# Positions and half of the first weights loaded first, the residual sum placed between the last query transposes, and the last down weights and the output in pieces

## The reference, cut to what matters

```python
# block 1: x + merged @ w_out, from three attention branches; two of them rotate by position angles
cos_a, sin_a = rope_tables(positions, A_ROT)
kv_m = rms_norm(mem, g_mem) @ w_mem_kv
# block 2
h = h + _mixer(...)
# cross attention
q = _rmsnorm((u @ w_q).reshape(b, s, 4, 256), qn)
k = _rmsnorm(kv[..., :d].reshape(b, m, 4, 256), kn)
h = h + (softmax(q @ k.T / 16) @ v) @ w_out
# experts
hid = silu(xb @ w_gate[e]) * (xb @ w_up[e])      # 1024 -> 512, for the rows routed to e
h = h + gate * (hid @ w_down[e])                 # 512 -> 1024
```

## Time and profile before

| | us |
|---|---|
| median of 3 runs | 1191.72 |
| lowest and highest run | 1190.08, 1197.29 |
| profiled execution | 1191.71 |
| its span, first to last instruction | 1189.8 |
| TensorE busy | 967.1 |
| vector engine busy | 314.9 |
| ScalarE busy | 174.0 |

### The profile page before, as it was taken

One profiled execution on the slowest core, in us unless ns is written; L12 is line 12 of the kernel. 1 busy time (PEld: TensorE's weight loads), 2 busy tenths in 40 slices (PEclk: granted clock), 3 DMA queues, 4 the chain that ended last, 5 costly groups with the idle time before them and its releaser, 6 DMA issues.

```text
span 1189.8 us, 10271 instructions
## 1 busy us (share of the span) xinstructions
PE 967.1 (81%) x4175; PEld 485.3 (41%) x4176; DVE 314.9 (26%) x835; ACT 174.0 (15%) x380; POOL 39.6 (3%) x93
## 2 busy tenths in 40 slices
PE   7999998899999899999899899756566565656555
PEld 3445484754444446455544555312131212121211
DVE  2316915623110421423654434101010101010100
ACT  2114223432000012211221222000000000000000
POOL 1012110000100010100000000000000000000000
PEclk9999999989999999999899999968697878697878
DMA  9455242303440744433206737999999999999993
GB/s 325 132 174 180 106 142 81 132 1 141 142 141 1 249 146 146 170 105 140 72 1 215 284 142 283 420 429 427 427 429 427 427 428 429 426 429 429 426 427 128
DMA packets 61981, 290.23 MB, mean 244 GB/s; under 512 B 8743, under 2 KB 11630, under 8 KB 49646
## 3 DMA queue, kind: packets, MB, share of 16 engines
q1 hardware_dynamic: 61934, 289.57, 61.5%
HBM read 288.51 MB, written 1.05 MB: 243 GB/s over the span
## 4 chain that ended last, share of the span: by engine, by line
PE 62%; DMA 28%; DVE 4%; SPq 3%; issue 1%; ACT 1%; DVEq 0%; ACTq 0%
PE ACC L480 32%; PE AUX L946 7%; DMA ring<-in_w_e_gate_dram 5%; PE ACC L494 5%; DMA ring<-in_w_e_down_dram 5%; PE ACC L513 4%; PE AUX L971 3%; DMA SQE<-in_w_e_up_dram 3%; DMA BIG<-in_w_e_up_dram 3%; DMA SQE<-in_w_e_down_dram 2%; DMA PJ<-in_w_e_up_dram 2%; DMA PJ<-in_w_e_down_dram 2%; DMA BIG<-in_w_e_gate_dram 2%; PE ACC L849 2%; DMA SQE<-in_w_e_gate_dram 2%; PE AUX L524 2%
## 5 line engine op out<-in xcount | busy, mean ns | idle before, releaser
L480 PE MATMUL ACC<-ring,BIG 128*128 128x512 f32 (+2 forms) x736 | 314.0, 587 | 4.1 <-ACT R L1280 2.5
L480 PEld LDWEIGHTS ACC<-ring,BIG 128*128 128x128 f32 x736 | 140.6, 192 | 169.7 <-issue 162.4
L946 PE MATMUL AUX<-ring,R 128*32 128x512 f32 x416 | 117.0, 727 | 52.2 <-DMA BIG<-in_w_e_up_dram 20.2
L480 PE MATMUL ACC<-ring,R 128*128 128x512 f32 (+1 forms) x232 | 100.9, 593 | 3.3 <-DMA ring<-in_w_mem_kv_dram 2.0
L946 PE MATMUL AUX<-R 128*32 128x512 f32 x112 | 63.5, 732 | 23.1 <-DMA ring<-in_w_e_gate_dram 13.0
L946 PE MATMUL AUX<-BIG,R 128*32 128x512 f32 x192 | 55.4, 742 | 27.7 <-DMA PJ<-in_w_e_up_dram 20.9
L971 PE MATMUL AUX<-ring,BIG 128*32 128x512 f32 x192 | 54.2, 728 | 19.0 <-DMA SQE<-in_w_e_down_dram 13.2
L946 PE MATMUL AUX<-PJ,R 128*32 128x512 f32 x192 | 54.2, 729 | 17.2 <-DMA ring<-in_w_e_up_dram 10.4
L2008 DVE SCALAR_TENSOR_TENSOR R<-R,AUX 128x512 f32<-128x512 f32 x8 | 5.5, 688 | 235.0 <-ACT R L1464 235.0
L480 PEld LDWEIGHTS ACC<-ring,R 128*128 128x128 f32 x232 | 44.6, 194 | 55.5 <-issue 55.2
L946 PEld LDWEIGHTS AUX<-ring,R 128*32 128x32 f32 x416 | 28.7, 130 | 92.5 <-issue 92.5
(11 more groups left out here) (292 smaller groups left out, 1047.7 us busy)
## 6 DMA issues: line engine op xcount, KB each, us to landing
ring<-in_w_in_dram SPq DMA_DIRECT2D x20, 2048.0 KB, 7.9
ring<-in_w_e_gate_dram SPq DMA_DIRECT2D x14, 2048.0 KB, 27.5
ring<-in_w_e_up_dram SPq DMA_DIRECT2D x12, 2048.0 KB, 30.2
ring<-in_w_e_down_dram SPq DMA_DIRECT2D x12, 2048.0 KB, 31.6
PJ<-in_w_e_down_dram SPq DMA_DIRECT2D x8, 2048.0 KB, 31.7
BIG<-in_w_e_up_dram SPq DMA_DIRECT2D x8, 2048.0 KB, 32.5
PJ<-in_w_e_gate_dram SPq DMA_DIRECT2D x6, 2048.0 KB, 26.6
BIG<-in_w_e_down_dram SPq DMA_DIRECT2D x6, 2048.0 KB, 27.4
```

The lines of the kernel that those rows point to most:

```text
L480: mm = nc.tensor.matmul(bank[:, t * 512:t * 512 + width], lhs[:, i, t * P:(t + 1) * P], w[:, i, a:a + width], start=(i == 0), stop=(i == k ...
L946: mm = nc.tensor.matmul(bank[r, :], M_xt[:, k, r], w[e][:, k, :], start=(k == 0), stop=(k == KD - 1))
```

## The change

1. The positions are loaded behind the gains, and the vector engine works out the angles before it drains the transposes of x, waiting for their own semaphore.
2. The first chunk, `mk`, is loaded in two halves of four 128-row blocks, and its product starts with the first.
3. The keys' transposes move ahead of the third query product. The last two query transposes stand apart, and between them the residual sum of one ACC tile and the scores of head 0.
4. `count_before(0)` stands ahead of the last blocks of the output product.
5. The down weights of the last group are loaded as 16 slices (block k of each expert) and the product takes them by block.
6. In the last group each half is copied when it is done, one by ScalarE and one by the vector engine; the place product closes the sums itself; the output is copied and stored by halves. The flag of the overflow branch is read earlier by ScalarE and the vector engine.

```diff
@@ project
-                wait_chunk(name)
+                if name == "mk":
+                    pe.wait_ge(first_landed, 16)
+                else:
+                    wait_chunk(name)
...
+                        if (name, t, i) == ("mk", 0, 4):
+                            wait_chunk(name)
@@ tensor, queries
                 elif (t, h) == (1, 0):
                     wait_turned("x2", [1])
+                    pe.wait_ge(heads_normed, 9)
+                    for k in range(TT):
+                        for g in range(2):
+                            turn(2 * k + g, ("xk", k, g))
                 elif (t, h) == (1, 1):
                     turn_queries(0)
...
-            pe.wait_ge(heads_normed, 9)
-            for t in range(TT):
-                for g in range(2):
-                    turn(2 * t + g, ("xk", t, g))
-            turn_queries(1)
-            wait_turned("xq")
-            wait_turned("xk")
...
-            start_sum(0)
-            attend("C", 0, 2)
-            start_sum(1)
+            first_sum = acc_no["wcq", 1, 0] % 2
+            pe.wait_ge(heads_normed, 12)
+            turn(2, ("xq", 1, 0))
+            start_sum(first_sum, ("wcq", 1, 0))
+            for t in range(TT):
+                wait_drained(pe, ("xq", t, 0))
+            wait_turned("xk")
+            attend("C", 0, 1)
+            pe.wait_ge(heads_normed, 13)
+            turn(3, ("xq", 1, 1))
+            start_sum(1 - first_sum, ("wcq", 1, 1))
+            attend("C", 1, 2)
+            wait_turned("xq")
@@ tensor, output product
-            add_wco(1, 1, range(4, KD)).then_inc(x3_done, 1)
+            add_wco(1, 1, range(4, 6))
             count_before(0)
+            add_wco(1, 1, range(6, KD)).then_inc(x3_done, 1)
@@ tensor, down product
                 for k in range(4):
+                    if g == GROUPS - 1:
+                        pe.wait_ge(row_landed[k], 16 * GROUP)
                     for h in range(2):
...
-                mm.then_inc(moe_down, 1)
+                        if k == 3:
+                            mm.then_inc(moe_down[h], 1)
                 for h in range(2):
                     pe.wait_ge(moe_out[h], g + 1)
...
+                        if last:
+                            mm.then_inc(y_done[h], 1)
...
-            for t in range(TT):
-                for h in range(2):
-                    mm = nc.tensor.matmul(ACC[t][:, h * 512:(h + 1) * 512], zeros_h[:, :],
-                                          causal[:, :].bitcast(BF16), start=False, stop=True, skip_group_check=True)
-            mm.then_inc(y_done, 1)
@@ sync
+            sp.dma_start(pos_i[:, :], A["positions"][0].rearrange("(t p) -> p t", p=P),
+                         allow_slow_non_contiguous=True).then_inc(pos_landed, 16)
...
+                    if c == 0:
+                        sp.dma_start(dst[:, 0:4, :], src[:, 0:4, :]).then_inc(first_landed, 16)
+                        dst, src = dst[:, 4:KD, :], src[:, 4:KD, :]
...
+            for k in range(4):
+                for e in range(GROUP):
+                    n = load_no(GROUPS - 1, 2, e)
+                    sp.dma_start(kt(stream[n % STREAM], 4)[:, k, :],
+                                 WD[(GROUPS - 1) * GROUP + e].rearrange("(p k) n -> p k n", p=P)[:, k, :]).then_inc(
+                        row_landed[k], 16)
...
-            for t in range(TT):
-                sp.wait_ge((out_ready, out_ready2)[t], 1)
-                sp.dma_start(out[0, t * P:(t + 1) * P, :], OUT[:, t, :]).then_inc(stored, 16)
+            for h in range(2):
+                for t in range(TT):
+                    sp.wait_ge(out_ready[t], h + 1)
+                    sp.dma_start(out[0, t * P:(t + 1) * P, h * 512:(h + 1) * 512],
+                                 OUT[:, t, h * 512:(h + 1) * 512]).then_inc(stored, 16)
@@ scalar, queries: inside the loop over (t, h), behind the copy of each product
-                if t:
-                    for k in range(TT):
-                        for h in range(2):
-                            drain_turned(("xk", k, h), CK8[:, 4 * h:4 * h + 4, :], 4)
-                for h in range(2):
-                    drain_turned(("xq", t, h), CQ8[:, 4 * h:4 * h + 4, :], 4)
+                    if (t, h) == (1, 0):
+                        for k in range(TT):
+                            for g in range(2):
+                                drain_turned(("xk", k, g), CK8[:, 4 * g:4 * g + 4, :], 4)
+                        for g in range(2):
+                            drain_turned(("xq", 0, g), CQ8[:, 4 * g:4 * g + 4, :], 4)
+            for g in range(2):
+                drain_turned(("xq", 1, g), CQ8[:, 4 * g:4 * g + 4, :], 4)
@@ vector
             norm_rows(1, X3, ZTv, 2)
-            drain_rows("x0", XT3, GC_NORM)
...
-            dve.wait_ge(small_landed, small_total)
+            dve.wait_ge(pos_landed, 16)
             link(v.tensor_copy(posf, pos_i[:, :]))
...
+            drain_rows("x0", XT3, GC_NORM)
+            dve.wait_ge(small_landed, small_total)
```

More of the change, by code:

```diff
@@ L199, in two_block_layer @@
         small_landed = sem("small_landed")
+        pos_landed = sem("pos_landed")
+        first_landed = sem("first_landed")
         x_landed = sem("x_landed")
@@ L253, in two_block_layer @@
         moe_tanh = sem("moe_tanh")
+        row_landed = [sem(f"row_landed{k}") for k in range(4)]
         moe_hidden = sem("moe_hidden")
@@ L431, in two_block_layer @@
             ("lambda_k2_2", GB_LAM + 192, 64))]
-        small += [(pos_i[:, :], A["positions"][0].rearrange("(t p) -> p t", p=P)), (GW[:, :], A["gla_gate_w_2"][0]),
+        small += [(GW[:, :], A["gla_gate_w_2"][0]),
                   (GF[:, :], A["norm_ffn_2"][0].rearrange("(p k) -> p k", k=KD))]
```

68 lines of the change are left out of this document (41 added, 27 removed).

## The result

| | before | changed |
|---|---|---|
| median, us | 1191.06 (4 runs) | 1172.66 (4 runs) |
| lowest and highest run | 1190.08, 1197.29 | 1171.72, 1173.98 |
| profiled execution (span) | 1191.71 (1189.8) | 1173.98 (1172.3) |

The ratio is 0.9846, with a 95% interval of 0.9824 to 0.9868: faster by 18.4 us, where 15.7 were forecast. Profiled execution against profiled execution it is 17.7 us.

What follows compares the result with a forecast made beforehand. TensorE's chain bounds the kernel to about 742 us, then a 427 GB/s stream without a hole, then what follows the last landing. Gains 4.7 + 2.2 + 0.5 + 8.3 = 15.7 us from 1191.71 gave 1176.0 us; range 1172 to 1182.

Steps and rivals of the forecast that it cites:

- Start: First products: 2.5 us of waiting, 1.7 of fallen clock and 0.5 from halved first weights go, 4.7 us gained.
- Queries: Query transposes and residual sums: idle pieces, lost clock and a rest go, less new waits, 2.2 us gained.
- (a): New wait: tile 0's query transposes wait 1.9 us while ScalarE, behind the third query product, empties a key bank.
- (b): New wait of 1.0 us for the last normalisation, after transpose, sum and head 0 fill 3.9 of 4.9 us.
- Ranking: Before the first gate product: counting tile 0's ranks earlier no longer holds back the vector engine's row copy, 0.5 us.
- Slices: Last down weights as 16 loads of 512 KB: the last landing comes 1.3 us later, between 0 and 3.0.
- End: After the last landing: shorter last product, copies and stores, no closing passes; -8.3 us including 1.3 of later landing.
- Swallowed head start: Rival: the gain at the start is lost between 50 and 740 us, giving 1180.7 us; chance 0.08.
- Clock falling at the new waits: Rival at the queries: TensorE idles 1.9 us and the clock falls, 1.7 us more, 1177.7 us; chance 0.14.
- Slow slices: Rival: last slices at 371 GB/s or a little under, 1.7 to 3.7 us more, 1178.7 us; chance 0.08.
- the fixed part of each transfer: Rival: 12 additional transfers each pay 1.9 us without overlap, 1198.8 us; 1.3 us each decides; chance 0.02.
- The better end: Rival: the clock stays up for the last quarter and slices cost nothing, 1173.0 us; chance 0.06.

Runs made afterwards that it cites:

- run 1: Changed kernel with the positions loaded third last of the small loads again and the angles behind the drain of x0: 1179.52 us.
- run 2: Changed kernel with the first weights again as one 2 MB load: 1171.88 us.
- run 3: Changed kernel with key and query transposes and both residual sums in the order of the kernel before, on TensorE and ScalarE: 1173.82 us.
- run 4: Changed kernel with the last group's down weights again as four 2 MB loads issued as early as before, output still by halves: 1181.72 us.
- run 6: Changed kernel with the other 92 expert weight loads also in four 512 KB pieces, 4 KB of each row: 1190.35 us.
- run 10: Changed kernel with six passes of zeros before the wait for the fourth slice of the last down product: 1171.83 us.
- run 12: Changed kernel with keys' banks emptied before ScalarE's wait for the third query product, and zero passes in the last wait and head waits: 1172.46 us.

## Why the prediction was right, step by step

- *Which part bounds what* held. The stream ran on at 427 GB/s, and each microsecond ahead of it moved it: gate product and last landing moved by 8.7 and 8.0 us.
- *Start, 4.7 us.* The wait of 2.5 us and the 1.7 us of clock behind it were right (46.82 to 44.26 us; run 1 gave back a wait and a fall). The halves' 0.5 us is 0.08 us in the changed kernel; against their own absence 0.2 us (run 2). I took the first product to begin where the vector engine ends; it begins 0.3 us later (11.98 to 12.29 us), and in this execution the vector engine itself was 0.26 us later than before. The positions' issue, priced at 0.4 us, moved the issue of the weights by 0.44.
- *Queries, 2.2 us.* 2.8 us in the trace (84.19 to 81.38 us), of which 0.6 is a shorter wait for a weight load that I had not counted. Waits (a) and (b) were foretold as 1.9 and 1.0 us and measured 1.76 and 0.81. The sum of 2.2 held 1.7 of clock and 0.5 of all the rest; run 3 has 1.7 and 0.3 (0.8 without the wait for the weights). So it pays by the clock, as forecast. Up to head 2's scores, the keys' transposes and their wait counted in, the traces have 12.3 us in place of 15.1, a gain of 2.8 where the sum has 2.7. From there to the `wco` passes it is 10.5 us against 10.1, the late vector engine that I had at 0.5.
- *Ranking, 0.5 us.* From the `wco` passes to the gate product: 44.33 us before, 43.90 in the traces whose clock stood there (runs 2, 3 and 4 among them), so 0.4 us. It is read between marks; no run took it back alone. In the changed kernel's own execution a fall hid it.
- *Ahead of the stream, 7.4 us* in the sum, 8.7 measured. The terms that are the edit's make 4.3 + 2.8 + 0.4 = 7.5. The rest, 1.2 us, is the clock: 1.7 us between 84 and 600 us, where the kernel before had six falls and the changed one four, at places that the diff doesn't touch, less 0.5 for the one in the ranking. It is no term of the change, but luck of the two executions.
- *Slices, 1.3 us.* 0.7 us in the last landing; run 6 makes 12 x 0.064 = 0.8 of it. The reason to take the lower part of 0 to 3.0 was right: the 371 GB/s belonged to a load that ran alone. What was not foreseen is the issue. Behind the first few SyncE was held up to 2 us for one load and needed until 1147.3 us for all sixteen, not 1146. With the last landing at about 1158 to 1161 us this cost nothing.
- *End, -9.6 us without the landing.* The last quarter was forecast at 3.4 us and took 3.5 (half clock); 1.85 us in runs 3, 10 and 12. So half speed was right for this execution and not for each, and the 1.7 us between the two are chance. Sum of the rest as forecast: 11.2 us from the last take to the end against 11.1. The closing passes (0.7 us) have no run of their own. Slices alone are worth 6.4 us net (run 4), forecast 5.0.
- *Rivals.* Swallowed head start: out (run 1). Clock falling at the new waits: did not come in any of the twelve traces with the new order. Slow slices and the fixed part of each transfer: out by run 6, which has 276 transfers more and loses 0.064 us each where 1.3 would have decided it. The better end (1173.0 us) lies nearest to the measured median, but it is not what happened in the traced execution: the last quarter ran at half clock, and the slices cost 0.7 us.

Of the 2.7 us between forecast and result the terms of the change make 0.6 (0.6 from the query weights and 0.6 from the slices, less 0.6 of start, ranking and end). In the profiled executions (17.5 us by their spans) the rest is the 1.2 us of clock ahead of the stream; the medians have another 0.9, which is scatter. So the mechanism was right term by term but for the halves, and the forecast's distance from the result is mostly chance.

## What to carry to other kernels

Read the windows behind each wait that an edit removes or adds: a fall of the clock costs up to 1.7 us here, so a wait of 2.5 us was worth 4.2 and an order of work that saves little waiting paid 1.7, while falls elsewhere scatter the medians by as much, so that small terms are read between two marks of the traces. Behind the last landing nothing overlaps, so the last load is split along the axis of the sum (two pieces do) and the output by halves. An engine that empties banks for another must not stand in a wait of its own ahead of them: the order of two drains in one queue was worth 2 us, as much as the whole reordering of the queries.

## What the runs showed of the hardware

- Queued transfers of 512 KB with 4 KB row pieces: 409 GB/s against 427 with whole 16 KB rows, at a full DMA share in both, 0.064 us for each transfer added.
- Queued transfers of 512 KB to 32 partitions: 219 GB/s at the same full share.
- The issue of a transfer is not always 0.43 us. In a full queue of 512 KB transfers SyncE is held for each as long as one takes to move:

```profile
918.06 10.20 SPq L1094 DMA_DIRECT2D BIG<-in_w_e_gate_dram  x8
```

  that is 1.28 us each, and 512 KB at 409 GB/s are 1.28 us. Anything else queued on SyncE would wait behind it (argued from its order, not shown).
- The 16 engines don't end together: in the last 4 us before the last landing their mean share was 0.44, falling from 0.78 to nothing, and 180 GB/s moved (window of the changed kernel). So the last slice waited 3.06 us for a tail and not for volume.

```profile
1157.00:1161.00 4.00, 1.06 (x12) 0.13 (x4) 0.00 (x0) 0.00 (x0) 0.00 (x0) 1.00 0.44 180
```
- Falls of the clock take 1.7 us or a multiple of it, and those of the table came behind short waits of TensorE (0.8 to 3.3 us), at some of them in one trace and not in another. The same wait of 1.75 us in the attention heads was followed by a fall at 184.68 us in the changed kernel and by none at 188.97 us in the kernel before.
